# Segment sums of an SSD layer: running sums split into bf16 parts and one bf16 matmul per head in place of a masked fp32 matmul

## What is computed

```
a_dt  = dt * a                              # per token and head
a_cs  = cumsum(a_dt)
seg   = a_cs[l] - a_cs[s]
decay = exp(where(l >= s, seg, -inf))
attn  = (C B^T) * decay
y_diag = attn @ (x * dt)
```

## Time and profile before

| | |
|---|---|
| runs, us | 1239.88, 1239.86, 1237.92; median 1239.86 |
| the profiled execution | 1236.62, its span 1234.9 |
| busy: TensorE, ScalarE, VectorE, GpSimd | 98%, 47%, 44%, 35% |
| granted TensorE clock | 0.999 |

### The profile page before, as it was taken

One profiled execution on the slowest core, in us unless ns is written; L12 is line 12 of the kernel. 1 busy time (PEld: TensorE's weight loads), 2 busy tenths in 40 slices (PEclk: granted clock), 3 DMA queues, 4 the chain that ended last, 5 costly groups with the idle time before them and its releaser, 6 DMA issues. The chain is left out here.

```text
span 1234.9 us, 16478 instructions
## 1 busy us (share of the span) xinstructions
PE 1206.3 (98%) x6267; PEld 934.9 (76%) x6267; DVE 544.3 (44%) x989; ACT 578.4 (47%) x1224; POOL 434.9 (35%) x243
## 2 busy tenths in 40 slices
PE   8999989999999999999999999999999999999998
PEld 7988845578988666678888877787666667878886
DVE  4211565553310555553476645800777760032333
ACT  6345556644443655554634432534556552332242
POOL 5543401114344222205344644344222224444451
PEclk9999999999999999999999999999999999999999
DMA  8433201203245999613322312233221113323231
GB/s 290 126 107 73 62 18 33 69 18 99 67 126 79 90 65 93 86 51 88 86 85 68 86 52 86 68 86 105 66 53 51 52 52 85 102 86 102 85 103 68
DMA packets 111406, 100.99 MB, mean 82 GB/s; under 512 B 21140, under 2 KB 98272, under 8 KB 111328
## 3 DMA queue, kind: packets, MB, share of 16 engines
q1 hardware_dynamic: 108784, 95.35, 33.3%
q0 software_dynamic: 864, 3.15, 0.7%
q10 hardware_dynamic: 1680, 1.44, 0.4%
HBM read 94.68 MB, written 2.10 MB: 78 GB/s over the span
## 5 line engine op out<-in xcount | busy, mean ns | idle before, releaser
L495 POOL TENSOR_TENSOR w_lo<-w_raw,w_hi 128x1024 fp32r<-128x1024 f32 (+6 forms) x169 | 380.3, 2251 | 727.6 <-ACT w_hi L490 727.6
L490 ACT ACTIVATE w_hi<-w_raw 128x1024 fp32r<-128x1024 f32 (+6 forms) x169 | 167.8, 993 | 261.3 <-PE bank L546 230.9
L546 PE MATMUL bank<-acts_hi,w_hi 128*128 128x512 f32 (+1 forms) x592 | 228.8, 386 | 3.9 <-POOL w_lo L495 2.3
L546 PE MATMUL bank<-acts_lo,w_hi 128*128 128x512 f32 (+1 forms) x592 | 227.1, 384 | 0.0
L546 PE MATMUL bank<-acts_hi,w_lo 128*128 128x512 f32 (+1 forms) x592 | 227.0, 383 | 0.0
L546 PEld LDWEIGHTS bank<-acts_hi,w_hi 128*128 128x128 f32 x592 | 111.2, 188 | 29.0 <-issue 5.2
L546 PEld LDWEIGHTS bank<-acts_lo,w_hi 128*128 128x128 f32 x592 | 111.2, 188 | 22.1
L546 PEld LDWEIGHTS bank<-acts_hi,w_lo 128*128 128x128 f32 x592 | 111.3, 188 | 21.3
L546 PE MATMUL bank<-w_hi,acts_hi 128*128 128x512 f32 (+4 forms) x308 | 109.3, 355 | 4.0 <-POOL w_lo L495 1.7
L1862 DVE TENSOR_TENSOR_SCAN arena_end<-arena 128x512 f32<-128x512 f32 (+3 forms) x64 | 80.8, 1263 | 63.1 <-ACT arena L1810 63.1
L546 PE MATMUL bank<-w_lo,acts_hi 128*128 128x512 f32 (+4 forms) x308 | 108.4, 352 | 0.0
(11 more groups left out here) (255 smaller groups left out, 2064.6 us busy)
## 6 DMA issues: line engine op xcount, KB each, us to landing
w_raw<-in_w_in SPq DMA_DIRECT2D x64, 512.0 KB, 3.7
w_raw<-in_w_out SPq DMA_DIRECT2D x24, 512.0 KB, 3.7
w_raw<-in_w_in_b SPq DMA_DIRECT2D x22, 512.0 KB, 5.1
w_raw<-in_w_in_a SPq DMA_DIRECT2D x10, 512.0 KB, 3.7
w_raw<-in_w_mem_kv SPq DMA_DIRECT2D x8, 512.0 KB, 8.6
w_raw<-in_w_sb_proj SPq DMA_DIRECT2D x8, 512.0 KB, 3.4
w_raw<-in_w_ssd_proj SPq DMA_DIRECT2D x8, 512.0 KB, 3.4
arena_shared<-junk SPq DMA_DIRECT2D x11, 256.0 KB, 20.4
```

The costliest lines, as they stand in the source:

```text
L490: nc.scalar.activation(w_at(p)[0][:, 0:size], w_raw[p % RAW][:, 0:size], ACT.Copy).then_inc(w_high.sem, 1)
L495: nc.gpsimd.tensor_tensor(lo[:, 0:size], w_raw[p % RAW][:, 0:size], hi[:, 0:size].bitcast(F32), ALU.subtract).then_inc(w_rest.sem, 1)
L546: mm = nc.tensor.matmul(bank_of(S, s, g)[0:lhs.shape[1], 0:rhs.shape[1]], lhs, rhs, start=j + kk + t == 0, stop=j == len(S.pieces) - 1 and ...
```

## The change

The segment sums are computed as a difference of running sums.

- On GpSimd, in layer 2 (`choose_pool`), a small 0/-1/+1 pattern `chosen` is made, and `tri_mid`, which is `tri_le` less its column for the chunk's middle, so that the running sum is taken from the middle of the chunk.
- On TensorE, after the first pair of chunks of `pC_x` (`sum_steps`): the three sum matmuls of before and a fourth one with `tri_mid`, into a bank that the projection does not use.
- On VectorE (`split_sums`): the fourth result is cut into three bf16 parts that add up to it exactly.
- On ScalarE, after the first pair (`choose`): `seg_key` rows 0 to 63 and `seg_query` rows 64 to 79 are filled from `chosen`, as bf16.
- After the second pair: TensorE turns the parts to rows with 4 + 16 bf16 matmuls against an identity (`turn_parts`), ScalarE moves them into the other rows of `seg_query` and `seg_key` in five copies (`collect_parts`).
- In the head loop: one bf16 matmul of 80 rows and 512 columns, `seg_key[:, n]` against `seg_query`, gives the negated segment sum. ScalarE clamps it at zero (Relu) from PSUM into `att`, and then takes the exponential in place with scale -1. The values above the diagonal become 1 and are masked by `c_sc` as before. TensorE may overwrite the bank after the clamp.
- `segD` and its 16 GpSimd products are gone; the DMA of the norm's gain, which stood behind them, goes out at the start of `ssd_pool`.
- The exponential of the sums takes its input from SBUF and waits for the parts.

```diff
-def turns(eng, n, emit):
+def turns(eng, n, emit, after=(None, None)):
     emit(0, False)
+    if after[0]:
+        after[0]()
     if n > 2:
         with eng.Fori(1, n - 1) as k:
             emit(k, False)
+    if after[1]:
+        after[1]()
     if n > 1:
         emit(n - 1, True)
...
+            def choose():
+                act.wait_ge(sem["chosen_made"], 1)
+                nc.scalar.activation(seg_key[0:HD], chosen[0:HD, 0:C_H].unsqueeze(2).to_broadcast([HD, C_H, P]),
+                                     ACT.Copy).then_inc(sem["seg_in"], 1)
+                nc.scalar.activation(seg_query[HD:SEG_ROWS],
+                                     chosen[HD:SEG_ROWS, C_H:C_H + MB].unsqueeze(2).to_broadcast([4 * MB, MB, P]),
+                                     ACT.Copy).then_inc(sem["seg_in"], 1)
+
+            def collect_parts():
+                for n, b in enumerate(SEG_BANKS):
+                    act.wait_ge(sem["parts_turned"], n + 1)
+                    if n == 0:
+                        nc.scalar.activation(seg_query[0:HD].rearrange("p m l -> p (m l)"), bank[b][0:HD, :],
+                                             ACT.Copy).then_inc(sem["seg_in"], 1)
+                    nc.scalar.activation(seg_key[HD:SEG_ROWS, 4 * n:4 * n + 4].rearrange("p h s -> p (h s)"),
+                                         bank[b][HD:SEG_ROWS, :], ACT.Copy).then_inc(sem["seg_in"], 1)
+            project_act(act, S, take, after=(choose, collect_parts))
...
-            act.wait_ge(sem["sums"], 1)
-            nc.scalar.activation(cut(23552 + 5 * 64, 3 * MB * C_H), bank[OB][:, 0:3 * MB * C_H],
-                                 ACT.Exp).then_inc(sem["ssd_ready"], 1)
+            act.wait_ge(sem["acs_parted"], 1)
+            nc.scalar.activation(acs_sums, acs_sums, ACT.Exp).then_inc(sem["ssd_ready"], 1)
...
-                    nc.scalar.activation(att[n % 2].rearrange("p m l -> p (m l)"), bank[OB + n % 2][:, :],
-                                         ACT.Exp).then_inc(sem["ssd_exp"], 1)
+                    fall = att[n % 2].rearrange("p m l -> p (m l)")
+                    nc.scalar.activation(fall, bank[OB + n % 2][:, :], ACT.Relu).then_inc(sem["ssd_fall"], 1)
+                    act.wait_ge(sem["ssd_fall"], n + 1)
+                    nc.scalar.activation(fall, fall, ACT.Exp, scale=-1.0).then_inc(sem["ssd_exp"], 1)
...
+            def sum_steps():
+                pe.wait_ge(sem["ssd_dt"], 2)
+                pe.wait_ge(sem["chosen_made"], 1)
+                for n, w in enumerate((tri_le, ones, tri_gt, tri_mid)):
+                    mm = nc.tensor.matmul(bank[SEG_BANKS[2]][:, n * 64:(n + 1) * 64], w[:, :],
+                                          dtA.rearrange("p m h -> p (m h)"), start=True, stop=True)
+                mm.then_inc(sem["sums"], 1)
+
+            def turn_parts():
+                pe.wait_ge(sem["acs_parted"], 1)
+                for m in range(MB):
+                    nc.tensor.matmul(bank[SEG_BANKS[0]][0:HD, m * P:(m + 1) * P], acs_parts[:, m].rearrange("p a h -> p (a h)"), ident_b[:, :],
+                                     start=True, stop=True)
+                for n in range(C_H):
+                    mm = nc.tensor.matmul(bank[SEG_BANKS[n // 4]][HD:SEG_ROWS, n % 4 * P:(n % 4 + 1) * P],
+                                          acs_parts.rearrange("p m a h -> p (m a) h")[:, :, n], ident_b[:, :], start=True, stop=True)
+                    if n % 4 == 3:
+                        mm.then_inc(sem["parts_turned"], 1)
+            project_pe(pe, pC_x, also=(sem["ssd_dt"], 1), after=(sum_steps, turn_parts))
...
-                    pe.wait_ge(sem["ssd_seg_in"], n + 1)
                     if n >= 2:
-                        pe.wait_ge(sem["ssd_exp"], n - 1)
-                    nc.tensor.matmul(bank[OB + n % 2][:, :], tri_gt[:, :], segD[n % 2].rearrange("p m l -> p (m l)"),
+                        pe.wait_ge(sem["ssd_fall"], n - 1)
+                    nc.tensor.matmul(bank[OB + n % 2][:, :], seg_key[0:SEG_ROWS, n],
+                                     seg_query[0:SEG_ROWS].rearrange("p m l -> p (m l)"),
                                      start=True, stop=True).then_inc(sem["ssd_seg"], 1)
...
+            def split_sums():
+                dve.wait_ge(sem["sums"], 1)
+                nc.vector.memset(acs_parts[:, :, PARTS], 0.0)
+                nc.vector.tensor_copy(acs_sums, bank[SEG_BANKS[2]][:, 0:3 * MB * C_H])
+                left_over = (bank[SEG_BANKS[2]][:, 3 * MB * C_H:4 * MB * C_H].rearrange("p (m h) -> p m h", m=MB), acs, c_u)
+                for a in range(PARTS):
+                    if a:
+                        link(nc.vector.tensor_tensor(left_over[a], left_over[a - 1], acs_parts[:, :, a - 1], ALU.subtract))
+                    ins = nc.vector.tensor_copy(acs_parts[:, :, a], left_over[a])
+                    if a < PARTS - 1:
+                        link(ins)
+                ins.then_inc(sem["acs_parted"], 1)
+            chunk_turns(dve, S, emit, (split_sums, None))
```

More of the change, by code:

```diff
@@ L231, in build @@
         w_raw = [sb(f"w_raw{n}", [P, PIECE]) for n in range(RAW)]
+        with nc.sbuf_tensor("seg_words", [P, 4 * D], BF16) as seg_words:
+            pass
         hn = sb("hn", [P, 2, D])
+        chosen = sb("chosen", [P, C_H + MB])
+        tri_mid = sb("tri_mid", [P, P])
         junk = sb("junk", [P, D])
@@ L399, in project, with chunk_turns @@
                               banks_free=banks_free, evac=C["evac"].take(n * groups) if evac else None, heads=heads, by_block=by_block, parts=parts)
-        def chunk_turns(eng, S, emit):
+        def chunk_turns(eng, S, emit, after=(None, None)):
             def both(k, last):
@@ L407, in chunk_turns @@
                 assert S.n % 2 == 0 and S.turn % RAW == 0
-                turns(eng, S.n // 2, both)
+                turns(eng, S.n // 2, both, after)
             else:
@@ L516, in project_pool, with project_pe @@
             chunk_turns(pool, S, emit)
-        def project_pe(pe, S, acts=None, ready=None, between=None, turns_in=(), also=None):
+        def project_pe(pe, S, acts=None, ready=None, between=None, turns_in=(), also=None, after=(None, None)):
             if S.banks_free > 0:
@@ L553, in emit, with project_act @@
                     between(s)
-            chunk_turns(pe, S, emit)
-        def project_act(act, S, take=None, first=None, between=None, freed=None, split=0):
+            chunk_turns(pe, S, emit, after)
+        def project_act(act, S, take=None, first=None, between=None, freed=None, split=0, after=(None, None)):
             def emit(k, s):
@@ L580, in emit @@
                     freed(last)
-            chunk_turns(act, S, emit)
+            chunk_turns(act, S, emit, after)
         norm_stages = []
@@ L1494, in ssd_pe @@
                 mm.then_inc(sem["ssd_sc"], 1)
-            pe.wait_ge(sem["ssd_dt"], 2)
             pe.wait_ge(sem["xT_out"], XT)
[L1497 to L1501, removed]
+            pe.wait_ge(sem["seg_in"], 3 + len(SEG_BANKS))
             for n in range(C_H + 1):
                 if n < C_H:
-                    pe.wait_ge(sem["ssd_seg_in"], n + 1)
                     if n >= 2:
-                        pe.wait_ge(sem["ssd_exp"], n - 1)
-                    nc.tensor.matmul(bank[OB + n % 2][:, :], tri_gt[:, :], segD[n % 2].rearrange("p m l -> p (m l)"),
+                        pe.wait_ge(sem["ssd_fall"], n - 1)
+                    nc.tensor.matmul(bank[OB + n % 2][:, :], seg_key[0:SEG_ROWS, n],
+                                     seg_query[0:SEG_ROWS].rearrange("p m l -> p (m l)"),
                                      start=True, stop=True).then_inc(sem["ssd_seg"], 1)
@@ L1558, in ssd_pool, with choose_pool @@
         def ssd_pool(pool):
[L1559 to L1570, removed]
             pool.dma_start(G_SSD, i["ssd_norm_2"].partition_broadcast(P)).then_inc(gain_in.sem, 16)
-            for n in range(done, LAST_SLOT):
+            for n in range(LAST_SLOT):
                 beside_pool(pool, n)
+        def choose_pool(link):
+            nc.gpsimd.tensor_tensor(tri_mid[:, :], tri_le[:, :], tri_le[:, P // 2 - 1:P // 2].to_broadcast([P, P]),
+                                    ALU.subtract)
+            link(nc.gpsimd.memset(chosen[:, :], 0.0))
+            for a in range(PARTS):
+                link(nc.gpsimd.affine_select(out=chosen[:, 0:C_H], in_=chosen[:, 0:C_H], pattern=[[-1, C_H]],
+                                             compare_op=ALU.not_equal, fill=-1.0, base=-C_H * a, channel_multiplier=1))
+            for a in range(PARTS):
+                ins = nc.gpsimd.affine_select(out=chosen[:, C_H:C_H + MB], in_=chosen[:, C_H:C_H + MB],
+                                              pattern=[[-4, MB]], compare_op=ALU.not_equal, fill=1.0,
+                                              base=-HD - a, channel_multiplier=1)
+                if a < PARTS - 1:
+                    link(ins)
+            ins.then_inc(sem["chosen_made"], 1)
```

(1 more changed line is left out.)

16 lines of the change are left out of this document (11 added, 5 removed).

## The result

| | before | after |
|---|---|---|
| median of 6 runs each, side by side, us | 1237.30 | 1232.02 |
| lowest and highest, us | 1236.29, 1239.88 | 1229.55, 1233.21 |
| profiled execution and its span, us | 1236.62, 1234.9 | 1233.21, 1231.5 |

The account below looks back on a forecast made before the run. TensorE, busy 98% of the span, bounds the kernel. Thirteen heads 8.2, burst -0.7, entry and additions -0.9, split heads -0.3 give 6.3 us off the 1239.86 median: 1233.6 us, own range 1231.5 to 1235.5, wider range 1230.0 to 1237.8.

Parts of the forecast that it names:

- The segment matmul: TensorE, each head: bf16 takes 0.22 us instead of 0.85, saving 0.63 a head, 10.1 for 16.
- The rival that bf16 would take the 0.85: Heads: the 80-row, 512-column bf16 product is no faster than fp32; 1242.1 us, chance 0.05.
- The entry: Before the first head: TensorE no longer waits for the sums and their exponential; 1.21 us removed.
- Additions: Convolution projection, TensorE: four fp32 sum matmuls cost 0.93 us, 20 bf16 turning matmuls 1.2.
- The turning: Convolution projection: 20 bf16 matmuls turning the parts to rows cost TensorE 1.2 us, at most 2.1.
- What was costed at nothing: Projection: added ScalarE copies (2.6 us per group) and small VectorE and GpSimd work fit idle time, costing nothing.
- copies slower: Projection: ScalarE's copies take double or triple the row price; 1237.6 us, mostly around 1235, chance 0.05.
- Heads with a split: Heads with a weight split in front: VectorE's product runs late beside GpSimd; 0.3 us in all (0 to 1).
- Splits hit harder: Heads with weight splits: diagonal product late by 0.5 us, at worst 3.5 over seven splits; 1236.8, chance 0.12.
- The burst: Silu burst, segment matmul 11 to diagonal product 12: ScalarE sets the pace, 11.81 us instead of 11.11, a 0.7 loss.
- No burst in the way: Silu burst: a ScalarE pass is hidden after all, so the gain is 9.2 us; 1230.7, chance 0.10.
- The rival on the other side: Heads: clamp and exponential share no table, so ScalarE loads twice a head; 1249.2 us, chance 0.04.

Follow-up runs that it names:

- e1: Changed kernel with its 16 segment matmuls back in fp32, on other data: 1238.45 us, ratio 1.0013 to the kernel before.
- e3: Changed kernel with the 20 bf16 matmuls that turn the parts issued twice: 1232.46 us, ratio 0.9959 to the kernel before.
- e6: Changed kernel with ScalarE's 2048-element fill of the key matrix done twice: 1233.02 us, ratio 0.9948 to the kernel before.
- e7: Changed kernel with ScalarE's 2048-element fill of the key matrix done four times: 1234.71 us, ratio 0.9972 to the kernel before.
- e5: Changed kernel with the eight Silus behind the heads and no Relu clamp (decays of 1): 1227.29 us, ratio 0.9903 to the kernel before.
- e4: Changed kernel with the eight Silus of z moved behind the last head: 1228.17 us, ratio 0.9928 to the kernel before.
- e9: The changed kernel run once more, nothing altered: 1231.11 us, ratio 0.9948 to the kernel before.
- e8: Changed kernel with ScalarE doing the four left Silus twice, a longer burst: 1234.81 us, ratio 0.9988 to the kernel before.
- e2: Changed kernel without the Relu clamp (decays of 1, VectorE takes a minimum with 1): 1232.36 us, ratio 0.9953 to the kernel before.
- e10: Changed kernel with the eight Silus behind the heads, run a second time: 1226.44 us, ratio 0.9909 to the kernel before.

## Why the prediction was right, point by point

**The segment matmul: as forecast.** 0.85 to 0.22. The row of after shows the pitch, 707.17 to 710.61, 3.44 against the forecast 3.4 (4.07 - 0.63 = 3.44), and e1 takes it back. The product after next starts at 707.64, 0.47 behind the segment matmul, where the prediction's sign was 0.45. The nearest row, two bf16 matmuls of 128 columns, was a good base for one of 512. The rival that bf16 would take the 0.85 is out.

**The entry: as forecast.** From the score matmuls to segment matmul 0 it was 690.48 - 687.49 = 2.99 and is 695.12 - 693.34 = 1.78: 1.21 less, the size on record.

**Additions: the sums right, the turning too small.** Between 635.21 and 636.02 lie the four sums, 0.81, and the product behind them takes 0.31 for 0.23: 0.89 (0.93 forecast). The turning: the product at 657.71 would have had its successor at 657.94, and the pair behind them is 0.33 apart and not 0.23; 659.71 - 0.23 - 657.94 = 1.54, forecast 1.2. Each costs 0.068 and not 0.055, as e3 shows by doubling, and 0.2 are entry and exit. This term was mis-sized by 0.34: the row of layer 2 had weights of 128 columns, these have 64 and 16, and no row of before had such a shape. Whether the shape is the reason no run tells. The bound of 2.1 held.

**What was costed at nothing: right in the result, wrong in its reason.** ScalarE's copies are about as forecast, 1.89 and 0.62, and 2.03 with 0.57 before it (2.6 forecast for each group):

```profile
637.75 1.89 ACT L1403 ACTIVATE seg_words<-chosen 64x2048 bf16<-64x2048 f32 x1
639.66 0.62 ACT L1405 ACTIVATE seg_words<-chosen 16x512 bf16<-16x512 f32 x1
641.76 1.06 ACT L504 ACTIVATE w_hi<-w_raw 128x1024 fp32r<-128x1024 f32 x1 [1.48 <-PE bank L560]
...
660.47 0.57 ACT L1413 ACTIVATE seg_words<-bank 64x512 bf16<-64x512 f32 x1
661.07 2.03 ACT L1415 ACTIVATE seg_words<-bank 16x512 bf16<-16x512 f32 x4
665.16 1.06 ACT L504 ACTIVATE w_hi<-w_raw 128x1024 fp32r<-128x1024 f32 x1 [2.07 <-PE bank L560]
```

ScalarE still idles 1.48 and 2.07 before the next split. But the sentence "a miss of up to 1.9, and with the 0.9 to 1.2 up to 3, costs nothing" does not hold. In e6 the split behind the copies is 0.5 late and TensorE loses 0.45; in e7 it is 4.4 late (645.70, where 641.34 was its place) and TensorE loses 4.22, not 2.7. I had followed the split directly behind the copies, and not the one after it, which hangs on a convolution and a Silu and whose w_lo has 0.2 in hand. The rival "copies slower" would have begun much sooner than I had it. It did not begin, as the copies are at the forecast price.

**Heads with a split: 0.3 forecast, 0 measured.** e5 equals e4, and the waits of after name none. VectorE's product, which took up to 2.49 beside GpSimd before, takes at most 1.84 in after and stays inside the 4.84 that TensorE leaves. "Splits hit harder" is out.

**The burst: right place, right mechanism, 0.5 too dear.** ScalarE's timeline after answers to the earlier trace rows:

```profile
731.67 0.60 ACT L1434 ACTIVATE arena_end<-bank 128x512 f32<-128x512 f32 x1 [2.18 <-PE bank L1552]
732.30 0.63 ACT L1436 ACTIVATE arena_end<-arena_end 128x512 f32<-128x512 f32 x1
732.95 1.28 ACT L1491 ACT_TABLE_LOAD   x1
...
739.20 0.61 ACT L1434 ACTIVATE arena_end<-bank 128x512 f32<-128x512 f32 x1
739.83 1.28 ACT L1436 ACT_TABLE_LOAD   x1
741.12 0.63 ACT L1436 ACTIVATE arena_end<-arena_end 128x512 f32<-128x512 f32 x1
```

VectorE's product behind it, after and then before:

```profile
741.79 0.69 DVE L1682 TENSOR_TENSOR arena_end<-arena_end,arena_shared 128x512 f32<-128x512 f32 x1 [6.50 <-ACT arena_end L1436]
```

```profile
743.55 1.07 DVE L1620 TENSOR_TENSOR arena_end<-arena_end,arena_shared 128x512 f32<-128x512 f32 x1 [5.32 <-ACT arena_end L1403]
```

The order is as I read it from the queue: both passes of head 11, load, banks and Silus, split, clamp of head 12, load, exponential. Forecast 11.81 from segment matmul 11 to diagonal product 12, measured 11.28; idle 3.2 forecast, 1.07 + 1.56 = 2.63 recorded. Of the 0.53, 0.38 is VectorE's product, which took 1.07 in the profile of before and takes 0.69 here. The forecast had left it at its old length. The remaining 0.15 is spread over the short overlaps of ScalarE's passes; no run singles it out. "No burst in the way" is out: e4 shows the burst costs 3.03.

**The sum.** Heads: forecast -8.4, and 0.53 (burst) and 0.3 (splits) better, -9.2; measured -9.25. Projection: +2.13, and 0.34 worse for the turning, 0.04 better for the sums: +2.43, measured +2.37. Misses of +0.8 (burst and splits) and -0.3 (turning and sums) left 6.3 near 6.88. That the ratio says 6.2, within 0.1 of the forecast, is luck. The six runs of before and the six of after do not lie on the levels in equal shares: two of before and three of after are some 3.5 above their lowest, and one of each is some 1.5 above. That takes 0.6 from the difference of the means, and the clock was in no step of the prediction. A gain larger by 0.6 and a draw worse by 0.6 offset each other.

**The rival on the other side** needed a table load between clamp and exponential. There is none in an ordinary head. The one at 739.83 is the burst's own, and the clamp at 739.20 ran under the table of Silu. The Trainium skill, ScalarE: Activation LUTs, section Table sets: the hidden batching unit, says that relu is in every set; this trace agrees, by the clamp at 739.20.

## What to carry to other kernels

Where one engine is busy all through, a removed piece is worth the distance of two starts on that engine, and e1 shows how exact this is; what eats the gain is the one place where another engine already sets the pace, and a pass that costs nothing in ordinary heads is paid for when it falls there (here the burst cost 3.03 us, 2.1 of them new, and all were gone when the Silus were moved behind the heads). Slack has to be followed through every chain that starts behind the added work, and not only to the next instruction of its queue: by the nearest rows a split could be 3 us late at no cost, and 0.5 us already cost 0.45. Before two spans are compared, look at the granted clock by stretches, and compare between like starts.

## What the runs showed of the hardware that was not expected

**The clock falls behind a short idle time, in some executions only.** In five profiled executions whose heads are the same code (after, e3, e6, e7, e9) TensorE idled twice in the burst, for 1.1 and 1.6 us; in four the granted clock behind it was between its levels of 1.2 and 2.4 GHz (0.70 in e3, 0.68 in e9, 0.93 over 735 to 760 us in e6 and e7) and the heads took 1.57 more; in the fifth it stayed at 1.00. With 1.07 and 4.21 (e8) it was 0.51, cost 2.47, and no run came near the 1232.2 that it would take without. With 0.41 and 1.40 (e2), in e1, e5, e4, e10 and in before it stayed at 1.00. So 2.63 us of idle time cost 3.03, and 4.6 where the clock fell. The other executions say that the fall is less frequent than four of five: of the twelve of after and e9 four lie near 1231.1, where it would put them (the profiled one of e9 is one of these; the others can also have the small form of the earlier fall, below), and none near 1234.7, where both falls together would. What decides it in one execution and not in the next is open.

**An earlier fall, in changed and unchanged code alike.** From 170 to 180 us the clock was 0.66 in after, e2, e5, e6 and e7, 0.83 in e10, 1.00 in before, e1, e3, e4, e8 and e9. In front of it TensorE had idled 0.9 and 1.5 us in every one of the twelve, whether the clock fell or not. From 171 to the norm of layer 3 TensorE took 2.9 to 3.2 more where it was 0.66 (3.16 in after) and 1.6 in e10. These steps fit the levels of the runs of before, near 1236.4, 1237.9 and 1239.9, and so do their granted clocks over the whole span, 0.999 or 1.000, 0.998 and 0.996; no execution of before at an upper level was profiled. Nothing in this study touches it.

**A wait costs more than its idle time.** Between segment matmul 11 and diagonal product 12, less the recorded idle time, lie 8.65 (after), 8.66 (e2) and 8.66 us (e8), but 8.25 in e4, where there is no wait: 0.4 for two waits, 0.2 each. In the projection 0.17 of recorded idle time cost 0.45 (e6), and 3.69 in two waits cost 4.22 (e7), about 0.27 a wait in both. No run tells what the extra time is.
